# The eight blocks of XH and of XL: 260 columns apart instead of 256

## The reference

```python
for l in range(DEPTH):                       # first_block, DEPTH = 2
    h = _rmsnorm(x, mix_norm[l])
    x = x + _mixer(h, w_in[l], ...)          # gated delta rule and HGRN2, both directions
    h = _rmsnorm(x, ffn_norm[l])
    x = x + _conv_ffn(h, w_up[l], ffn_conv[l], ffn_conv_bias[l], w_down[l])
...
for layer in range(DEPTH):                   # second_block
    hn = rms_norm(h, norm_attn[layer])
    h = h + (nsa_mixer if layer < 1 else swa_sink_mixer)(hn, ...)
    h = h + conv_ffn(rms_norm(h, norm_ffn[layer]), ffn_w_in[layer], ...)
return rms_norm(h, final_norm)
```

## Time and profile before

| what | us |
|---|---|
| median of three runs | 1676.87 |
| lowest and highest | 1676.51, 1679.12 |
| span of the profiled execution | 1673.4 |
| TensorE busy (matmuls) | 1625.0 |
| VectorE busy | 1218.8 |
| ScalarE busy | 989.4 |
| share of TensorE in the chain that ended last | 81% |

### The profile page before, as it was taken

One profiled execution on the slowest core, in us unless ns is written; L12 is line 12 of the kernel. 1 busy time (PEld: TensorE's weight loads), 2 busy tenths in 40 slices (PEclk: granted clock), 3 DMA queues, 4 the chain that ended last, 5 costly groups with the idle time before them and its releaser, 6 DMA issues.

```text
span 1673.4 us, 29412 instructions
## 1 busy us (share of the span) xinstructions
PE 1625.0 (97%) x12534; PEld 1549.8 (93%) x12534; DVE 1218.8 (73%) x1715; ACT 989.4 (59%) x1494; POOL 7.9 (0%) x14
## 2 busy tenths in 40 slices
PE   8999899999999999899999999999999999899998
PEld 7999899999989999899999988878999988799997
DVE  7889736777758789646777657766688758678864
ACT  7775555556546784565566542356677645567753
POOL 0000000000000000000000000000000000000000
PEclk9999999999999999999999999999999999999999
DMA  7422125455554412126555552620455544055551
GB/s 272 171 77 77 51 77 201 160 195 200 178 200 151 151 54 77 51 76 227 179 194 182 186 187 104 228 75 2 167 186 179 200 176 158 1 202 189 189 191 62
DMA packets 35843, 246.04 MB, mean 147 GB/s; under 512 B 4096, under 2 KB 4480, under 8 KB 6656
## 3 DMA queue, kind: packets, MB, share of 16 engines
q1 hardware_dynamic: 35712, 244.15, 41.1%
HBM read 243.09 MB, written 1.05 MB: 146 GB/s over the span
## 4 chain that ended last, share of the span: by engine, by line
PE 81%; DVE 11%; ACT 5%; issue 1%; DMA 1%; SPq 0%; DVEq 0%; ACTq 0%
PE PS L402 81%; DVE SB L1753 2%; DVE SB L1762 2%; DVE WL L1753 2%; ACT SB L1111 2%; DVE SA L1753 2%; ACT WH L1114 1%; DVE SB L2006 1%; DVE SB L2010 1%; PE PS L405 1%; DMA RAW<-w_in 0%; DVE SA L1920 0%; ACT SB L1691 0%; DVE SA L1762 0%; ACT SA L1111 0%
## 5 line engine op out<-in xcount | busy, mean ns | idle before, releaser
L402 PE MATMUL PS<-XH,WH 128*128 128x256 f32 (+1 forms) x2536 | 714.5, 282 | 10.8 <-DVE WL L1753 6.7
L402 PE MATMUL PS<-XL,WH 128*128 128x256 f32 (+1 forms) x2536 | 712.9, 281 | 0.0
L402 PE MATMUL PS<-XH,WL 128*128 128x256 f32 (+1 forms) x2536 | 712.5, 281 | 0.0
L1114 ACT CAST WH<-RAW 128x2048 fp32r<-128x2048 f32 (+1 forms) x229 | 427.0, 1865 | 399.1 <-PE PS L402 364.1
L1753 DVE TENSOR_TENSOR WL<-RAW,WH 128x2048 fp32r<-128x2048 f32 (+1 forms) x229 | 511.5, 2234 | 124.4 <-ACT WH L1114 120.3
L402 PEld LDWEIGHTS PS<-XH,WH 128*128 128x128 f32 (+1 forms) x2536 | 477.1, 188 | 15.6 <-issue 6.0
L402 PEld LDWEIGHTS PS<-XL,WH 128*128 128x128 f32 (+1 forms) x2536 | 475.2, 187 | 2.7 <-issue 1.9
L402 PEld LDWEIGHTS PS<-XH,WL 128*128 128x128 f32 (+1 forms) x2536 | 474.9, 187 | 0.3
L402 PE MATMUL PS<-INHL,WH 128*128 128x512 f32 (+1 forms) x1216 | 334.7, 344 | 1.2 <-DVE INHL L1753 1.2
L402 PE MATMUL PS<-INHL,WL 128*128 128x256 f32 x960 | 270.0, 281 | 0.0
L402 PEld LDWEIGHTS PS<-INHL,WH 128*128 128x128 f32 x1216 | 210.3, 188 | 29.2 <-ACT INHL L1114 1.5
(11 more groups left out here) (142 smaller groups left out, 1456.7 us busy)
## 6 DMA issues: line engine op xcount, KB each, us to landing
RAW<-w_in SPq DMA_DIRECT2D x51, 1024.0 KB, 4.8
RAW<-w_up SPq DMA_DIRECT2D x44, 1024.0 KB, 4.7
RAW<-f_in SPq DMA_DIRECT2D x44, 1024.0 KB, 4.7
RAW<-w_down SPq DMA_DIRECT2D x22, 1024.0 KB, 4.8
RAW<-f_out SPq DMA_DIRECT2D x22, 1024.0 KB, 4.7
RAW<-a_w_in SPq DMA_DIRECT2D x10, 1024.0 KB, 4.7
RAW<-w_out SPq DMA_DIRECT2D x8, 1024.0 KB, 4.9
RAW<-w_bdn SPq DMA_DIRECT2D x4, 1024.0 KB, 4.9
```

Of the source, the lines that this page charges most:

```text
L402: return e.matmul(out, l, r, start=start, stop=stop, skip_group_check=True)
L1114: e.copy(out, x).then_inc(*A.up(*key, of=of))
```

## The change

`XH` and `XL` become 8 x 260 columns wide, and block k starts at column 260k. All places that address a block go through a new function `blk`. Each block still has 256 columns that are used; the four columns between two blocks are read and written by nobody. `MZ` leaves the constants, so that `C` is 1502 columns wide instead of 1630. `XH2`, `XL2`, `X` and `INHL` keep their 256 columns.

```diff
-    ["ident", "TU", "TL", "MF", "MZ", "MB", "MP", "ROT"])}
-CN_COS, CN_SIN = 8 * 128, 8 * 128 + 256
+    ["ident", "TU", "TL", "MF", "MB", "MP", "ROT"])}
+CN_COS, CN_SIN = 7 * 128, 7 * 128 + 256
...
-        XH = sb("XH", 2048, R)
+        XH = sb("XH", 8 * 260, R)
         PR = sb("PR", P_W)
-        XL = sb("XL", 2048, R)
+        XL = sb("XL", 8 * 260, R)
...
+        STEP = {id(XH): 260, id(XL): 260}
...
+        def blk(x, k):
+
+            at_ = k * STEP.get(id(x), 256)
+            return x[:, at_:at_ + 256]
...
-                        x = slice((xo + k) * 256, (xo + k) * 256 + 256)
+                        x, y = blk(xh, xo + k), blk(xl, xo + k)
...
-                            mm(o, wh[:, s], xh[:, x], k == 0 and j == 0, False)
-                            mm(o, wh[:, s], xl[:, x], False, False)
-                            last = mm(o, wl[:, s], xh[:, x], False, k == nk - 1)
+                            mm(o, wh[:, s], x, k == 0 and j == 0, False)
+                            mm(o, wh[:, s], y, False, False)
+                            last = mm(o, wl[:, s], x, False, k == nk - 1)
...
-                        s, x = slice(k * 256, k * 256 + 256), slice(k * 256 + j * 128, k * 256 + j * 128 + 128)
-                        pairs.append((XH[:, x], XL[:, x], wh[:, s], wl[:, s]))
+                        s, x = slice(k * 256, k * 256 + 256), slice(j * 128, j * 128 + 128)
+                        pairs.append((blk(XH, k)[:, x], blk(XL, k)[:, x], wh[:, s], wl[:, s]))
...
-                    e.mul(halves_of(st)[0][:, s], X[:, s], norm_gain(st, k)).then_inc(*A.up("x hi", st, k))
+                    e.mul(blk(halves_of(st)[0], k), X[:, s], norm_gain(st, k)).then_inc(*A.up("x hi", st, k))
...
-                stt(xl[:, s], X[:, s], norm_gain(st, k), xh[:, s].bitcast(F), ALU.mult, ALU.subtract, "x lo", st, k)
+                stt(blk(xl, k), X[:, s], norm_gain(st, k), blk(xh, k).bitcast(F), ALU.mult, ALU.subtract, "x lo", st, k)
...
-    put("MZ", 0.0)
```

More of the change, by code:

```diff
@@ L33 @@
 CN = {n: i * 128 for i, n in enumerate(
-    ["ident", "TU", "TL", "MF", "MZ", "MB", "MP", "ROT"])}
-CN_COS, CN_SIN = 8 * 128, 8 * 128 + 256
-CN_CC, CN_CS = 8 * 128 + 512, 8 * 128 + 527
-CN_CM, CN_CV = 8 * 128 + 542, 8 * 128 + 542 + 32
+    ["ident", "TU", "TL", "MF", "MB", "MP", "ROT"])}
+CN_COS, CN_SIN = 7 * 128, 7 * 128 + 256
+CN_CC, CN_CS = 7 * 128 + 512, 7 * 128 + 527
+CN_CM, CN_CV = 7 * 128 + 542, 7 * 128 + 542 + 32
 CN_W = CN_CV + 32
@@ L474, in narrow @@
                 for k in range(8):
-                    s, x = slice(k * width, k * width + width), slice(k * 256, k * 256 + 256)
-                    pairs.append((wh[:, s], wl[:, s], XH[:, x], XL[:, x]))
+                    s = slice(k * width, k * width + width)
+                    pairs.append((wh[:, s], wl[:, s], blk(XH, k), blk(XL, k)))
                 tri(p[0:width, 0:256], pairs, st).then_inc(*P.up("ps", *key))
```

## The result

The changed kernel takes 1679.42 us (median of 13 runs, 1677.8 to 1682.22), the kernel before 1675.7 us (13 runs, 1673.2 to 1679.12). The medians are 3.7 us apart. The ratio is 1.0025, with a 95% interval of 1.0018 to 1.0033: by it the changed kernel is slower by 4.2 us, where 1676.7 us and no change were forecast. The profiled execution took 1678.64 us with a span of 1676.9; that of before has a span of 1673.4.

What follows compares the result with a forecast made beforehand. TensorE was taken as the bound, mostly a count of matmuls times their pace of 117.9 ns. 1673.4 - 0.15 = 1673.25 us span, with 3.5 us around it 1676.7 us; range 1666 to 1687 us.

Steps and rivals of the forecast that it cites:

- step 3: Moving operand of `feat` starting 1040 bytes on per block instead of 1024: pace stays 117.9 ns, +-0 (bounds -40, +314 us).
- rival B: Slower pace: moving starts 16 bytes past a multiple of 32, or changing position, cost 6.4 us: 1683.1; chance 0.29.
- step 4: Other operands (INHL, XH2, XL2) show two paces, 1.1 ns apart, for the same addresses; XH and XL show the slower.
- A: Faster pace: spacing breaks the pattern of 15, XH and XL streams reach 116.7 ns, -7.1 us: 1669.6; chance 0.31.
- C: Change doesn't do what it says: starts are multiples of 16, not 8 past one; 1676.7, chance 0.40 shared with forecast.
- step 5: Tensors behind XL stand 256 bytes lower: INHL's streams could change pace, at most 2.4 us either way; taken as 0.
- step 1: Constants shrink by 65,536 bytes, shortening their transfer at the start: -0.15 us, or 0 if the chain waits for ScalarE.

## Why the prediction was wrong

The step that failed is step 3, the term for the new operand starts: I took +-0 because columns, type, weights and order stay. It measured 1.06 ns on each matmul that moves XH or XL, 4.0 us on the chain, and so passed the sign that I had set, a move of the pace by more than 0.5 ns. What the runs show is that the pace of these fp32r streams depends on the starts of the moving blocks against those of the weights, modulo 256 bytes. In the up-projections it moves between 116.7 and 120 ns with them, both ways, and in shorter streams between 113.3 and 121.2. +-0 lay inside that spread and was not worked out from anything.

**The place asked about.** Step 3 and rival B looked at starts 16 bytes past a multiple of 32. That is not it: with all blocks on such starts the ratio is 1.0005. The larger part is a by-product: XH became 128 bytes wider, XL's first block went from place 32 to 160, and that pair runs at 119.3 ns with a step of 256 (two runs). The step of 1040 bytes then walks through the places in steps of 16, and the pace becomes a mean over them: 118.8 with this start, 118.1 with the old one. In the first up-projection of the changed kernel the six matmuls of a block are on the mean 118.3, 119.0, 118.7, 119.7, 119.5, 119.9, 117.4 and 118.3 ns apart, block by block. Taking MZ out shifted XH by 512 bytes, two whole periods; the run with everything 256 bytes higher says that such a shift changes no pace. In step 4 I had the numbers for a better question: XH's and XL's distance modulo 1024, before and after, and two paces for the same addresses. I compared modulo 1024, while INHL's place of 160 against XL's of 32, which only modulo 256 shows, was not looked at.

**The rivals.** B's end was right, and its price of 1 ns on the mean was close to the 1.06 measured by luck. Of its two mechanisms the first, starts 16 bytes past a multiple of 32, is not it. The blocks on such starts are 0.75 ns slower on the mean in the changed kernel, as B's sign has it, but with the step of 260 at the old starts they are 0.3 ns faster (117.9 against 118.2), so the sign comes from the places. The second, a position that changes from block to block, holds for 0.3 ns. Its 6.4 us were 2.2 too many against the 4.2 measured (the time of 1683.1 us was 3.7 too high, in part because 13 runs put the kernel before at 1675.7 us), and the weight was mis-sized: I put 6400 matmuls on the path. The four up-projections hold 4224 of them, 1.06 x 4224 = 4.5 us, and the chain pays 3.97 us there, 4.4 against the second profile of before. The 2176 in mixers and attention brought nothing that these profiles show apart from their noise, although their paces did rise (118.5 ns and more in most streams). That a slower stream there shortens a wait of TensorE for others would explain it, but was not tested, and it does not hold in general: with the step taken back, at 119.3 ns, 3.8 of the 9.9 us lay outside the four pieces. A, the faster pace, exists and holds 0.35%, but needs the blocks in one good place, and the step of 260 is what forbids that. C was right as a remark on the words and had no part in the time.

**What held.** INHL did not slow down (step 5): three of its four long streams kept 116.7 ns, and the one that the earlier trace rows has at 118.0 went to 116.7, as it did in the second profile of the kernel before, so this is no effect of the change. The writes of XH and XL stayed at 0.50 and 0.48 us:

```profile
L1160 ACT ACTIVATE XH<-X,PR x64: 492/497/512, 3.9 to 1480.3; 128x256 fp32r<-128x256 f32 x64
L1768 DVE SCALAR_TENSOR_TENSOR XL<-X,PR,XH x64: 475/484/490, 4.5 to 1480.8; 128x256 fp32r<-128x256 f32 x64
```

The smaller constants (step 1) brought the landing at the start from 8.20 to 7.95 us, against 0.15 us expected. In the profiles whose chain waits for this landing it took 8.20 to 8.77 us in five kernels with MZ and 7.67 to 8.02 us in six without it, which agrees with the sign and leaves the size open. The range, 1666 to 1687 us, held the time. The measurement was also sharper than the 0.2% that I gave: with 13 runs the interval is 0.15% wide.

The Trainium skill, "SBUF — State Buffer", section "SBUF: two separate sides", has the two reads of TensorE independent of each other, and step 3 took from it that the new spacing does nothing. The run in which, of what these streams read, only WH and WL moved, by 128 bytes, went from 117.8 to 120.0 ns in three streams, so here the measurement decides: how the two operands stand to each other counts. The 109.2 ns that step 3 took from the Trainium skill, "TensorE: Matmul & The Clock Gate", section "Back-to-back issue gap", is given there as the gap of a single matmul; for a stream of pairs of weight load and matmul the section lets both set the spacing. The lowest pace of such a stream of 256 columns here was 113.3 ns.

## What to carry to other kernels

A layout change can be a change of speed where TensorE runs back to back: note every operand's start modulo 256 bytes before and after, also of the tensors that only moved along, and read the pace of each kind of stream. It shows 0.1 ns, which is 0.4 us over the four up-projections, while single runs of the kernel before lie up to 5.9 us apart. In streams like these, keep block steps at a multiple of 256 bytes and then choose the start: that gave the best kernel (116.7 ns), and at a bad start also one slower than the padded step (119.3 against 118.8 ns). To weigh a change of pace, count the long streams that end in no wait; what short streams between waits add was near nothing in one run here and 3.8 us in another, so leave a range for it.

## What the runs showed of the hardware

For fp32r matmuls of 256 columns with a weight load of 128 columns before each, at a granted clock of 1.00, the mean distance from start to start keeps one value within a stream, to 0.1 ns, over up to 1019 matmuls where the step is a multiple of 256 bytes. Values that came again in several streams are 113.3, 116.7, 117.3, 117.8, 118.3, 118.7, 119.3 and 120.0 ns; the highest was 121.2. Places found, weights at 128: (160, 160) 116.7, in some streams of INHL and XH2 117.8 or 120.0; (96, 96) 118.3; (0, 96) 116.7; (0, 32), (32, 0), (160, 32) and (64, 64) 117.8; (192, 192) 117.8 or 113.3; (32, 32) 117.3, 118.7 or 120.0; (16, 176) 117.8 or 120.0; (0, 224) 118.5; (0, 160) 119.3; (0, 0), (128, 128) and (224, 224) 120.0; (0, 64) 117.7 or 121.1; (0, 128) 119.3 to 120.0. Most of these places were seen in one to four streams of one run, so other paces may exist there. A stream that mixes 512 and 256 columns of INHL ran at 173.5 ns at 160 and at 32, at 176.8 at 96, and at 174.6 or 176.8 at 192. Which process makes the paces is open; no run looked inside TensorE's reads. Open is also what picks between the paces of one place: the same kernel gave 117.8 and 116.7 ns in one INHL stream in two executions.
